# Expert products of the PEER layer: 72 pieces in the 512-column form, their two partial sums added by a DMA

## The chip, the cores and the metric

The kernel runs on one core of a Trainium2 chip. The metric is the device time of one launch in microseconds (us), median over runs. Engines are named as the profile does: PE (TensorE; PEld is its weight load), DVE (VectorE), ACT (ScalarE), POOL (GpSimd), SP (the engine that issues nearly all loads). SPq and POOLq are the DMA queues that SP and POOL issue to.

## What is computed

Three transformer blocks in float32 on 256 tokens of width 1024. The change touches the product with the first expert table in the feed-forward layer (PEER) of the second block:

```python
def peer_ffn(xn, w_q, keys1, keys2, u_tab, v_tab):
    q = (xt @ w_q).reshape(T, PEER_HEADS, PEER_QDIM)
    ...                                    # scores against two key sets, top 16 of each, top 16 of the sums
    gw = jax.nn.softmax(sv, axis=-1)
        u = jnp.take(u_tab, ec, axis=0)    # 16384 experts of 1024 numbers
        act = jnp.einsum('td,thkd->thk', xc, u).astype(f32)
        hact = (jax.nn.gelu(act, approximate=False) * gc).astype(xc.dtype)
        return jnp.einsum('thk,thkd->td', hact, jnp.take(v_tab, ec, axis=0))
```

The kernel gathers nothing. It multiplies all 16384 experts with all 256 tokens, takes the Gelu of every product, multiplies by a weight that is zero for experts not selected, and multiplies with all of the second table.

## The kernel before, in words

**Halves.** Every weight (`raw`, 1 MB chunks of two pieces, 128 x 1024 numbers each) is split for PE in two: ACT copies the rounded number to the high half (L2896, the `hi` of a piece), and DVE (L1543) or POOL (L1431, in `lower`) subtracts it from the weight, which gives the low half `lo`. The activations are kept as two halves as well, `XX`: high ones `xh`, low ones `xl`. A product is hi·xh + hi·xl + lo·xh. Pieces lie in a ring of four buffers `halves`; ACT makes the high half of piece n+3 when PE has read piece n-1. There are up to three `raw` slots; SP loads a slot again when both low halves of its chunk are made.

**The expert stage.** `peer` on PE first makes queries (pieces of the kind `wide`), then 64 small score products (L1246), and then loops over 128 pieces of the table, 128 experts each ("pr.u"). For each, `tile_mms` issues 8 times a product hi·xh (L585) and one hi·xl (L586), and then 8 of lo·xh (L589): 24 products of 256 columns. Two pieces share one of the four PSUM banks of `main`. ACT takes the Gelu of the two pieces at once from PSUM (L3547, `taken`) into `hidden`, 256 columns for each piece; `hidden` fills up to column 32768 of `AR`.

**The other form.** `wide` (used for the queries, and for the gated layers) keeps one bank for a piece. It issues 8 products of 512 columns (L747), which leave hi·xh and hi·xl side by side in the bank, 256 columns each, and 8 of 256 columns that add lo·xh to the first of them (L746); these 8 come before the last of the 512-column ones. The two halves of the bank are then to be added by someone. For the queries ACT copies one half and DVE adds the other.

**Beside the first 72 pieces** (`SELECTED = 72`) DVE selects: `select` does maxima and searches (L2453 to L2458) and then, for the last of it, additions and products of up to 2048 columns (L2480 to L2504), given out in portions of 1750 columns for each piece and finished at piece 72. For those pieces POOL makes the low halves of the odd ones (L1498, L1499), DVE the even ones. From piece 74 on, one-hot matrices are built by DVE, ACT and POOL (L1509), PE multiplies them ("pr.w", L1268), and the weights are applied; DVE makes all low halves from piece 72 on.

**Order.** Each engine runs its instructions in program order. ACT's loop (L3550 to L3567) does for each n: the high half of piece n+3, then for odd n the Gelu of pieces n-1 and n. POOL's loop only makes low halves. `Banks.take` makes PE wait until the bank's last use was emptied.

Of the kernel before, what the change touches and what calls it, by code (L numbers as in the profile page):

```python
# [7 lines left out]
F32 = mybir.dt.float32  # L8
# [3 lines left out]
ALU = mybir.AluOpType  # L12
ACT = mybir.ActivationFunctionType
# [8 lines left out]
SELECTED = 72  # L22
# [264 lines left out]
def weighed_before(f):  # L287

    return groups_of(f).stop
# [16 lines left out]
    "mm",  # L306
]
DMAS = ["ident_in", "cols_in", "const", "x_in0", "x_in1", "pin", "lam_in", "dist_in", "keys_in", "spilled", "refilled", "rg_in", "merge_in",
        "stored", "gb0", "gb1"]


class Program:
# [149 lines left out]
    def unit(self, q):  # L462

        return (self.first[:, 0, 0], self.first[:, 1, 0]) if q == 0 else (self.X[0][:, q % 8, :], self.X[1][:, q % 8, :])

    def hot(self):

# [41 lines left out]
def tensor_engine(k):  # L509

    nc, ps, X, d = k.nc, k.ps, k.X, k.d
    mm, transpose = nc.tensor.matmul, nc.tensor.transpose
    pe, main, aux, s = On(nc.tensor), k.main, k.aux, k.s
# [714 lines left out]
    def peer(prev):  # L1228
        turn_half("pr.x", prev, 0)
        rx = turned_x("pr.x")  # L1230
        B0 = 88 * 256
        qT, k1, k2 = k.ar(B0, 16, 256), k.ar(B0 - 2048, 8, 128), k.ar(B0 - 1024, 8, 128)
        first = four("pr.q", X, rx, lambda: turn_half("pr.x", prev, 1))
        for f in range(4, 16):
            wide(("pr.q", f), main, rx)
            if f == 5:
                turn_back("pr.q", first, (("pr.q", 0), ("pr.q", 2)))
        pe.wait_ge(*k.dma["keys_in"].need(2))
        for j in range(2):
            for sd in range(2):  # L1240
                for h0 in (0, 4):
                    b = main.take(pe, ("pr.s", j, sd, h0))
                    pe.wait_ge(*main.gone(("pr.q", 2)))
                    pe.wait_ge(*main.gone(("pr.q", 7 if h0 == 0 else 15)))
                    for h in range(h0, h0 + 4):
                        ins = mm(ps[:, b, (h - h0) * 128:(h - h0 + 1) * 128],  # L1246
                                 qT[:, 2 * h + sd, j * 128:(j + 1) * 128], (k1, k2)[sd][:, h, :],
                                 start=True, stop=True)
                    filled(("pr.s", j, sd, h0), ins)
        sel = k.AR[:, B0 + 3072:B0 + 3840].rearrange("p (w j n) -> p w j n", w=3, n=128)  # L1250
        OA, OB = k.hot()

        def selected():
            b0, b1 = aux.take(pe, ("pr", "sel", 0)), aux.take(pe, ("pr", "sel", 1))
            pe.wait_ge(*s["vec"].need("pr.sel"))
            for q in range(3):
                bb, oo = (b0, q * 256) if q < 2 else (b1, 0)
                for j in range(2):
                    ins = transpose(ps[:, bb, oo + j * 128:oo + j * 128 + 128], sel[:, q, j], ident[:])
            filled(("pr", "sel"), ins)  # L1260

        def weigh(g):
            b = aux.take(pe, ("pr.w", g))
            pe.wait_ge(*s["prob"].need(("pr.hot", g)))
            pe.wait_ge(*s["pool"].need(("pr.hot", g)))
            pe.wait_ge(*s["act"].need(("pr.hot", g)))
            for q in range(4):
                ins = mm(ps[:, b, q * 128:(q + 1) * 128], OB[:, g % 2, q, :], OA[:, g % 2, q, :],  # L1268
                         start=True, stop=True)
            filled(("pr.w", g), ins)  # L1270

        for n in range(128):
            if n % 2 == 0:
                b = main.take(pe, ("pr.u", n))
            m, hi, lo = weights()
            o = n % 2 * 256
            ins = tile_mms(ps[:, b, o:o + 256], m, hi, lo, X, 0, 8, True, True, rx)
            ins.then_inc(k.piece_read, 1)
            if n % 2:
                k.full["pr.u", n - 1] = k.piece_read, m + 1  # L1280
            if n == SELECTED:
                selected()
            for g in groups_of(n):
                weigh(g)
        down("pr", 128, X, lambda t: [s["part"].need(("pr.v", t))], ring=8)
# [131 lines left out]
def gpsimd_engine(k):  # L1417

    nc, d, dma, s = k.nc, k.d, k.dma, k.s
    gp = On(nc.gpsimd)  # L1420
    load = nc.gpsimd.dma_start
# [3 lines left out]
        gp.wait_ge(*need)  # L1425
        nc.gpsimd.tensor_tensor(dst, src, half[:, 0:src.shape[1]], ALU.pow).then_inc(*s["pow"].mark(name))  # L1426

    def lower(n):
        src, hi, lo = k.piece(n)
        gp.wait_ge(k.hi_made, n + 1)  # L1430
        nc.gpsimd.tensor_tensor(lo, src, hi.bitcast(F32), ALU.subtract).then_inc(k.lo_pool, 1)  # L1431

    def residual(key, row, more):
        def first(j):
# [24 lines left out]
    for h in range(4):  # L1459
        n = 2 * h  # L1460
# [28 lines left out]
    for g in range(8):  # L1489
        n = 2 * g  # L1490
# [4 lines left out]
    B0 = 88 * 256  # L1495
    for j in range(2):
        load(k.ar(B0 - 2048 + 1024 * j, 8, 128), d["keys"][j]).then_inc(*dma["keys_in"].mark(j + 1))
    for n in range(1, SELECTED, 2):  # L1498
        lower(k.u_first + n)  # L1499
    OA, OB = k.hot()  # L1500
    ih1, ih2, gw = k.xsel[:, 0:256], k.xsel[:, 256:512], k.xsel[:, 512:768]
    gp.wait_ge(*k.aux.gone(("pr", "sel", 1)))
# [25 lines left out]
def vector_engine(k):  # L1528

    nc, ps, X, st, x, XN, d = k.nc, k.ps, k.X, k.st, k.x, k.XN, k.d  # L1530
    v, main, aux, s, full = On(nc.vector), k.main, k.aux, k.s, k.full
    te = nc.vector
    step = s["vec"]
# [888 lines left out]
    def peer(prev):  # L2422
        B0 = 88 * 256
        act = k.ar(0, 128, 256)
# [128 lines left out]
        def weighed(g, m):  # L2553

            v.wait_ge(*full["pr.w", g])
            if not weighed_before(m - 2):
                v.wait_ge(*main.gone(("pr.u", m - 2)))
            w = ps[:, aux.of(("pr.w", g)), :].rearrange("p (t i) -> p i t", i=128)
            ts = slice(g * 4, g * 4 + 4)
            te.tensor_tensor(act[:, 0:m, ts], act[:, 0:m, ts], w[:, 0:m], ALU.mult)  # L2560
            te.tensor_copy(act[:, m:128, ts], w[:, m:128]).then_inc(*aux.done(("pr.w", g)))
# [317 lines left out]
def scalar_engine(k):  # L2879
# [624 lines left out]
    def peer(prev):  # L3504
# [33 lines left out]

        def taken(f):

            t = weighed_before(f) * 4
            p = two(main.of(("pr.u", f)))
            a.wait_ge(*full["pr.u", f])
            if t:
                ins = act(p[:, :, 0:t], p[:, :, 0:t], ACT.Gelu)
            if t < 256:
                ins = act(hidden[:, f:f + 2, t:256], p[:, :, t:256], ACT.Gelu)  # L3547
            ins.then_inc(*(s["act"].mark(("pr.h", f)) if t else main.done(("pr.u", f))))

        for n in range(128):  # L3550
            if n == FIRST_HOT - 1:
                a.wait_ge(*aux.gone(("pr", "sel", 1)))
                for need in k.chunk_halved(k.hot_after):
                    a.wait_ge(*need)
                hot(0)
            weights()
            if n == SELECTED - 2:
                w = k.AR[:, B0 + 1536:B0 + 1792]
                a.wait_ge(*s["vec"].need(("pr.sv", 1)))
                act(w, w, ACT.Exp).then_inc(*s["act"].mark("pr.exp"))  # L3560
            for g in groups_of(n):
                if g:
                    hot(g)
            if n == 1:
                a.wait_ge(*full["pr.s", 1, 1, 4])
            if n % 2 and n < 127:
                taken(n - 1)  # L3567
        a.wait_ge(*aux.gone(("pr.w", 63)))
        a.parts = 0
# [377 lines left out]
```

## Time and profile before

| | us |
|---|---|
| device time, median of 3 runs (2816.61 to 3042.89) | 2816.8 |
| span of the profiled execution | 2814.9 |
| PE busy | 2800.3 (99%) |
| DVE busy | 1952.1 (69%) |
| ACT busy | 1624.4 (58%) |
| POOL busy | 345.9 (12%) |

The span is one execution as the hardware profiler saw it; what the device time has beyond it lies before the first and after the last instruction. A share of busy time is an average over all three blocks; the expert stage with its 128 pieces lies from about 1520 to about 1945 us.

### The profile page before, as it was taken

The numbers are of one execution on the slowest core, as the hardware profiler recorded it, in microseconds if no ns is written. First come the engines' busy times: TensorE is split into PE (matmuls) and PEld (weight loads), VectorE is DVE, ScalarE is ACT, GpSimd is POOL, SyncE is SP. The second block draws the span as 40 slices with busy tenths as digits, with TensorE's granted clock in tenths as the row PEclk, the third lists the DMA queues.
The fourth block names the chain that finished last, engine by engine and source line by source line (L and its number), as shares of the span: only waits on it lengthen the run. The fifth ranks groups of instructions, "written<-read, shape, count | busy, mean of one in ns | idle before, by whom it ended". The sixth has DMA issues, their size and how long they took to land.

```text
span 2814.9 us, 42397 instructions
## 1 busy us (share of the span) xinstructions
PE 2800.3 (99%) x16834; PEld 2485.0 (88%) x16834; DVE 1952.1 (69%) x3377; ACT 1624.4 (58%) x2784; POOL 345.9 (12%) x314
## 2 busy tenths in 40 slices
PE   9999999999999999999999999999999999999999
PEld 7888888888988888899889999999888889988997
DVE  6657765776676676768866998677555566766775
ACT  6544655755665564566745445776555555655663
POOL 0000000000010002000002445894000000000000
PEclk9999999999999999999999999999999999999999
DMA  7554556466436555445164554434555574536454
GB/s 229 191 178 159 181 194 227 135 202 221 148 124 194 202 189 181 135 156 187 61 224 166 183 182 160 136 131 161 193 192 193 194 246 137 180 110 209 147 195 149
DMA packets 270485, 491.25 MB, mean 175 GB/s; under 512 B 10880, under 2 KB 181248, under 8 KB 261584
## 3 DMA queue, kind: packets, MB, share of 16 engines
q1 hardware_dynamic: 268864, 480.08, 51.3%
q0 software_dynamic: 1424, 8.45, 0.8%
q8 instruction: 135, 2.21, 0.3%
q14 instruction: 62, 0.51, 0.1%
HBM read 486.41 MB, written 2.10 MB: 174 GB/s over the span
## 4 chain that ended last, share of the span: by engine, by line
PE 94%; DVE 4%; ACT 1%; issue 0%; DMA 0%; POOL 0%; DVEq 0%; POOLq 0%; ACTq 0%
PE ps L659 41%; PE ps L747 11%; PE ps L589 8%; PE ps L585 8%; PE ps L586 8%; PE ps L746 6%; PE ps L606 3%; PE ps L1268 2%; DVE halves L1543 1%; PE ps L1303 1%; PE ps L544 1%; DVE AR L2499 1%; PE ps L952 0%; PE ps L1322 0%; DVE AR L2495 0%
## 5 line engine op out<-in xcount | busy, mean ns | idle before, releaser
L2896 ACT ACTIVATE halves<-raw 128x1024 fp32r<-128x1024 f32 x828 | 870.1, 1058 | 695.5 <-PE ps L659 413.7
L1543 DVE TENSOR_TENSOR halves<-raw,halves 128x1024 fp32r<-128x1024 f32 x790 | 952.9, 1227 | 190.6 <-ACT halves L2896 187.4
L659 PE MATMUL ps<-halves,XX 128*128 128x512 f32 x2628 | 611.6, 391 | 0.4
L659 PEld LDWEIGHTS ps<-halves,XX 128*128 128x128 f32 x2628 | 489.9, 188 | 102.5 <-DVE XX L1581 1.0
L585 PE MATMUL ps<-XX,halves 128*128 128x256 f32 (+1 forms) x1960 | 486.1, 286 | 0.0
L586 PE MATMUL ps<-XX,halves 128*128 128x256 f32 (+1 forms) x1960 | 480.3, 283 | 0.0
L659 PE MATMUL ps<-halves,R 128*128 128x512 f32 x1908 | 439.9, 390 | 0.1
L659 PEld LDWEIGHTS ps<-halves,R 128*128 128x128 f32 x1908 | 356.7, 188 | 73.9 <-issue 0.6
L586 PEld LDWEIGHTS ps<-XX,halves 128*128 128x128 f32 (+1 forms) x1960 | 375.4, 192 | 0.1
L585 PEld LDWEIGHTS ps<-XX,halves 128*128 128x128 f32 (+1 forms) x1960 | 375.0, 191 | 0.1
L747 PE MATMUL ps<-XX,halves 128*128 128x512 f32 x1344 | 338.4, 393 | 0.6 <-DVE XX L1581 0.6
L747 PEld LDWEIGHTS ps<-XX,halves 128*128 128x128 f32 x1344 | 241.7, 189 | 44.5 <-ACT halves L2896 0.9
L589 PE MATMUL ps<-XX,halves 128*128 128x256 f32 (+1 forms) x1960 | 275.3, 283 | 0.2 <-DVE halves L1543 0.2
L589 PEld LDWEIGHTS ps<-XX,halves 128*128 128x128 f32 (+1 forms) x1960 | 252.7, 192 | 0.4 <-DVE halves L1543 0.4
L746 PEld LDWEIGHTS ps<-XX,halves 128*128 128x128 f32 x1344 | 183.2, 190 | 13.4 <-issue 0.4
L746 PE MATMUL ps<-XX,halves 128*128 128x256 f32 x1344 | 187.5, 282 | 0.1
L1426 POOL TENSOR_TENSOR st<-st 128x1 f32<-128x1 f32 x44 | 25.3, 574 | 1182.0 <-DVE st L1608 1001.9
L1431 POOL TENSOR_TENSOR halves<-raw,halves 128x1024 fp32r<-128x1024 f32 x38 | 97.0, 2552 | 435.3 <-ACT halves L2896 435.3
L1558 DVE TENSOR_TENSOR XX<-AR,XX 128x256 fp32r<-128x256 f32 x127 | 53.9, 426 | 137.9 <-ACT XX L3579 137.9
L1509 POOL TENSOR_SCALAR raw<-iota,xsel 128x128 f32<-128x128 f32 x128 | 137.5, 1081 | 34.5 <-PE ps L1268 22.4
L1807 DVE TENSOR_TENSOR AR<-AR,ps 128x256 f32<-128x256 f32 x164 | 68.5, 421 | 81.1 <-ACT AR L3096 81.1
L3096 ACT ACTIVATE AR<-ps 128x256 f32<-128x256 f32 x164 | 61.3, 375 | 89.4 <-PE ps L747 88.0
(390 smaller groups left out, 3180.8 us busy)
## 6 DMA issues: line engine op xcount, KB each, us to landing
raw<-in_w_ffn_in SPq DMA_DIRECT2D x88, 1024.0 KB, 5.1
raw<-in_w_in SPq DMA_DIRECT2D x74, 1024.0 KB, 5.3
raw<-in_uT SPq DMA_DIRECT2D x64, 1024.0 KB, 4.9
raw<-in_peer_v SPq DMA_DIRECT2D x64, 1024.0 KB, 4.9
raw<-in_w_ffn_out SPq DMA_DIRECT2D x44, 1024.0 KB, 4.9
raw<-in_w_up SPq DMA_DIRECT2D x24, 1024.0 KB, 5.8
raw<-in_mlstm_w_in SPq DMA_DIRECT2D x12, 1024.0 KB, 5.2
raw<-in_w_down SPq DMA_DIRECT2D x12, 1024.0 KB, 4.9
```

Of the source, the lines that this page charges most:

```text
L585: mm(o[:, ts], hi[:, q, 0:M], xh[:, k0 + q, ts], start=first and q == 0, stop=False)
L586: mm(o[:, ts], hi[:, q, 0:M], xl[:, k0 + q, ts], start=False, stop=False)
L589: ins = mm(o[:, ts], lo[:, q, 0:M], xh[:, k0 + q, ts], start=False, stop=last and q == a - 1)
L606: ins = mm(ps[:, bs[j], :].rearrange("p (a b) -> p a b", b=128), act[q == 2][:, t, j * 128:(j + 1) * 128], k.halves[:, 0:4, q % 2, t * 128 ...
L659: ins = mm(ps[:, bs[j * (width // 512) + h], :], xv[:, k0 + t, j * 128:(j + 1) * 128], wv[:, t, h * 512:(h + 1) * 512], start=first and q ...
L746: mm(o[:, 0:256], lo[:, p, :], X[0][:, p, :], start=False, stop=False)
L747: ins = mm(o.rearrange("p (h t) -> p h t", t=256), hi[:, q, :], k.XX[:, :, q, :], start=q == 0, stop=q == 7)
L1431: nc.gpsimd.tensor_tensor(lo, src, hi.bitcast(F32), ALU.subtract).then_inc(k.lo_pool, 1)
L1509: nc.gpsimd.tensor_scalar(OA[:, g % 2, q, :], k.iota[:], ih1[:, 4 * g + q:4 * g + q + 1], gw[:, 4 * g + q:4 * g + q + 1], ALU.is_equal, AL ...
L1543: te.tensor_tensor(lo, src, hi.bitcast(F32), ALU.subtract).then_inc(k.lo_made, 1)
L1807: te.tensor_tensor(dst, dst, o[:, 0:256], ALU.add) \
L2896: act(hi, src, ACT.Copy).then_inc(k.hi_made, 1)
```

## The change

For the first 72 pieces PE uses `wide` in place of `tile_mms`. ACT copies the two halves of each bank to a ring for 8 pieces in `AR`, at columns that belong to pieces 72 to 87 of `hidden` (`sides`). For each pair of pieces POOL then issues a DMA from `AR` to `AR` that adds the one half to the other in memory (`summed`, `accum_op=ALU.add`, 256 KB in 1 KB rows, four semaphores in turn), and ACT takes the Gelu of the pair from there, 6 pieces after the pair began. POOL's low halves of the odd pieces are made in four instructions of 256 columns instead of one of 1024. DVE's first weighing no longer waits on a PSUM bank where the piece is one of the 72.

```diff
-        "stored", "gb0", "gb1"]
+        "stored", "u_sum0", "u_sum1", "u_sum2", "u_sum3", "gb0", "gb1"]
...
+    def sides(self, f):
+
+        return self.ar((SELECTED + f % 8 * 2) * 256, 2, 2, 256)
...
-        for n in range(128):
+        for n in range(SELECTED):
+            wide(("pr.u", n), main, rx)
+        for n in range(SELECTED, 128):
...
-    def lower(n):
+    def lower(n, step=8):
         src, hi, lo = k.piece(n)
         gp.wait_ge(k.hi_made, n + 1)
-        nc.gpsimd.tensor_tensor(lo, src, hi.bitcast(F32), ALU.subtract).then_inc(k.lo_pool, 1)
+        for q in range(0, 8, step):
+            ts = slice(q, q + step) if step < 8 else slice(None)
+            ins = nc.gpsimd.tensor_tensor(lo[:, ts], src[:, ts], hi[:, ts].bitcast(F32), ALU.subtract)
+        ins.then_inc(k.lo_pool, 1)
...
-    for n in range(1, SELECTED, 2):
-        lower(k.u_first + n)
+    def summed(f):
+        gp.wait_ge(*k.main.gone(("pr.u", f)))
+        gp.wait_ge(*k.main.gone(("pr.u", f + 1)))
+        parts = k.sides(f)
+        load(parts[:, :, 0], parts[:, :, 1], accum_op=ALU.add).then_inc(*dma[f"u_sum{f // 2 % 4}"].mark(f))
+
+    for n in range(1, SELECTED + 4, 2):
+        if n >= 5:
+            summed(n - 5)
+        if n < SELECTED:
+            lower(k.u_first + n, 2)
...
-                v.wait_ge(*main.gone(("pr.u", m - 2)))
+                v.wait_ge(*(main.gone(("pr.u", m - 2)) if m - 2 >= SELECTED else s["act"].need(("pr.h", m - 2))))
...
         def taken(f):
 
+            if f < SELECTED:
+                a.wait_ge(*k.dma[f"u_sum{f // 2 % 4}"].need(f))
+                act(hidden[:, f:f + 2, :], k.sides(f)[:, :, 0], ACT.Gelu).then_inc(*s["act"].mark(("pr.h", f)))
+                return
...
-            if n % 2 and n < 127:
+            if n % 2 == 0 and 6 <= n <= SELECTED:
+                taken(n - 6)
+            if 1 <= n <= SELECTED:
+                if n >= 9:
+                    a.wait_ge(*s["act"].need(("pr.h", n - 9 - (n - 1) % 2)))
+                a.wait_ge(*full["pr.u", n - 1])
+                act(k.sides(n - 1 - (n - 1) % 2)[:, (n - 1) % 2],
+                    ps[:, main.of(("pr.u", n - 1)), :].rearrange("p (h t) -> p h t", t=256), ACT.Copy) \
+                    .then_inc(*main.done(("pr.u", n - 1)))
+            if n == SELECTED + 1:
+                taken(SELECTED - 4)
+                taken(SELECTED - 2)
+            if n % 2 and SELECTED < n < 127:
                 taken(n - 1)
```

## Rows read from the trace of the kernel before

**Rows 1.** The page: span, then busy time (share) and instructions.

```profile
span 2814.9 us, 42397 instructions
PE 2800.3 (99%) x16834; PEld 2485.0 (88%) x16834; DVE 1952.1 (69%) x3377; ACT 1624.4 (58%) x2784; POOL 345.9 (12%) x314
```

**Rows 2.** Busy by window: stretch, length, each engine, PEclk, DMA share, GB/s.

```profile
1600.00:1640.00 40.00, 40.00 (x335) 40.00 (x335) 35.95 (x89) 18.26 (x21) 18.52 (x7) 1.00 0.55 185
1640.00:1680.00 40.00, 40.00 (x336) 40.00 (x335) 37.81 (x71) 18.26 (x21) 18.41 (x7) 1.00 0.56 185
1680.00:1720.00 40.00, 39.84 (x332) 39.57 (x331) 39.73 (x37) 17.79 (x21) 18.17 (x7) 1.00 0.51 171
1800.00:1840.00 40.00, 40.00 (x344) 40.00 (x343) 28.35 (x67) 31.46 (x73) 35.74 (x39) 1.00 0.40 133
```

**Rows 3.** Chain of work, 1490 to 1960, the longest pieces: start us, us, what.

```profile
1489.97 1.84 PE ps L747 x8
...
1509.53 1.84 PE ps L747 x8
...
1521.98 0.96 PE ps L589 x8
...
1651.58 0.96 PE ps L589 x8
...
1655.52 1.07 ACT halves L2896
...
1671.18 4.24 DVE AR L2499 x6
...
1712.34 1.21 PE ps L589 x8
```

**Rows 4.** Timeline of PE, 1698 to 1735: start us, us, then [idle before <-releaser].

```profile
1712.34 1.21 PE L589 MATMUL ps<-XX,halves 128*128 128x256 f32 x8 [0.16 <-DVE halves L1543]
...
1729.71 1.12 PE L589 MATMUL ps<-XX,halves 128*128 128x256 f32 x8
1730.67 0.82 PE L1259 MATMUL ps<-ident,AR 128*128 128x128 f32 x6
```

**Rows 5.** Timeline of ACT, 1580 to 1600, one pair of pieces.

```profile
1583.46 0.60 ACT L3547 ACTIVATE AR<-ps 128x512 f32<-128x512 f32 x1 [1.76 <-PE ps L589]
1583.95 1.05 ACT L2896 ACTIVATE halves<-raw 128x1024 fp32r<-128x1024 f32 x1
1586.40 1.06 ACT L2896 ACTIVATE halves<-raw 128x1024 fp32r<-128x1024 f32 x1 [1.40 <-PE ps L589]
```

**Rows 6.** Timeline of ACT, 1660 to 1745.

```profile
1737.33 1.06 ACT L2896 ACTIVATE halves<-raw 128x1024 fp32r<-128x1024 f32 x1 [0.82 <-PE ps L589]
```

**Rows 7.** Groups by line and form, ACT, 1480 to 1520: busy us, mean ns.

```profile
L3523 ACT ACTIVATE AR<-ps 128x512 f32<-128x512 f32 x7 | 4.2, 597 | 2.7 <-PE ps L1246 2.7
```

**Rows 8.** Timeline of POOL, 1400 to 1745.

```profile
1579.32 2.40 POOL L1431 TENSOR_TENSOR halves<-raw,halves 128x1024 fp32r<-128x1024 f32 x1 [3.36 <-ACT halves L2896]
...
1665.72 3.72 POOL L1431 TENSOR_TENSOR halves<-raw,halves 128x1024 fp32r<-128x1024 f32 x1 [3.35 <-ACT halves L2896]
...
1734.30 0.60 POOL L1511 TENSOR_SCALAR raw<-iota,xsel 128x128 f32<-128x128 f32 x1
```

**Rows 9.** Groups by line, POOL, whole span: busy us, mean ns | idle before.

```profile
L1426 POOL TENSOR_TENSOR st<-st 128x1 f32<-128x1 f32 x44 | 25.3, 574 | 1182.0 <-DVE st L1608 1001.9 <-DVE st L1629 173.9 <-DVE st L2814 6.3
...
L1464 POOL DMA_DIRECT2D AR<-in_pT x1 | 0.7, 739 | 1.5 <-DVE AR L1635 1.5
...
L1478 POOL DMA_DIRECT2D AR<-in_pT x1 | 0.6, 581 | 1.4 <-DVE AR L1635 1.4
```

**Rows 10.** DMA issues of the whole span: queue, count, KB each, median us to landing.

```profile
raw<-in_uT SPq DMA_DIRECT2D x64, 1024.0 KB, 4.9
...
AR<-in_pT POOLq DMA_DIRECT2D x2, 256.0 KB, 3.0
```

**Rows 11.** Instructions of the tile in_rg: the longest landing in the trace.

```profile
DMA to landing us min/median/max: 7.3/8.9/10.5
```

**Rows 12.** Timeline of DVE, 1655 to 1745.

```profile
1660.86 1.59 DVE L2487 TENSOR_SCALAR AR<-AR 128x128 uint32<-128x128 uint32 x1
1662.49 0.23 DVE L2489 TENSOR_SCALAR AR<-AR 128x128 uint32<-128x128 uint32 x1
...
1664.87 2.29 DVE L2495 TENSOR_TENSOR AR<-AR,iota 128x2048 f32<-128x2048 f32 x1
1667.20 2.85 DVE L2499 TENSOR_TENSOR AR<-AR 128x256 f32<-128x256 f32 x2
...
1700.26 4.31 DVE L2499 TENSOR_TENSOR AR<-AR 128x256 f32<-128x256 f32 x6
...
1711.06 1.23 DVE L1543 TENSOR_TENSOR halves<-raw,halves 128x1024 fp32r<-128x1024 f32 x1
...
1716.88 1.42 DVE L2499 TENSOR_TENSOR AR<-AR 128x256 f32<-128x256 f32 x4
...
1726.35 0.42 DVE L2518 TENSOR_TENSOR AR<-AR,st 128x256 f32<-128x256 f32 x1
```

## The prediction

> **What bounds the kernel now.** The page first: PE is busy for 2800.3 us of a span of 2814.9 [rows 1]. Anything that is to make this kernel faster has to take time from PE or from the few places where PE waits; anything else can only hurt. The windows of the expert stage say who is near PE: up to 1640 us DVE is busy for 36 of 40 us, in 1680:1720 for 39.73, and there PE shows its only loss, 0.16 us; ACT is at 18 and POOL at 18 of 40, the DMA engines at 0.55 [rows 2]. From 1800 on, where the change does nothing, POOL is the fullest after PE, but PE is full. Then the chain of waits: it runs on PE products throughout the stage, except between 1655.5 and 1712 us, where it goes over DVE's selection (L2499 and its like) and comes back to PE at 1712.34 [rows 3]. The timeline of PE has the wait itself: the low-half products of piece 66 start right behind DVE's low half, which ended at 1712.29 [rows 4, 12]. So the stage is PE's, with one stretch of some 57 us in which DVE has no time left over. The median of the runs, 2816.8 us, is 1.9 above the span; I make the sum on the span and add the 1.9.
>
> **PE, the gain.** A narrow piece: 45 pieces lie between the starts of the low-half products at 1521.98 and 1651.58, so 129.60 / 45 = 2.880 us. A piece in the 512-column form: 7 of them between 1489.97 and 1509.53, 19.56 / 7 = 2.794 us [rows 3]. Both stream the same columns (16 x 256 + 8 x 256 against 8 x 512 + 8 x 256); only the per-instruction loss of 8 products goes. 72 x 0.0857 = 6.2 us. This is the same code at the same granted clock of 1.00 a few us earlier in the same trace, so I take it as it is. It is also the whole possible gain, 0.2% of the time, apart from the stalls that stand there now: pieces 0 to 72 take 1729.71 - 1521.98 = 207.73 against 72 x 2.880 = 207.36 [rows 3, 4], 0.4 us.
>
> **DVE, what is given back.** From about piece 46 (the chain leaves PE at 1655.5; (1655.5 - 1522) / 2.88 = 46) to the low half of piece 66, DVE works without a gap. The change takes no work from DVE. Where PE paces DVE, before piece 46, DVE's 10% of idle time absorbs the faster PE; in the 20 pieces after, PE asks for them 20 x 0.0857 = 1.7 us sooner and doesn't get them. In the new form the low half is also wanted earlier within the piece, after 7 of 8 wide products, 7 x 0.23 = 1.61 us (1.84 / 8 = 0.23), in place of 16 x 0.12 = 1.92 us: 0.3 us. Together 2.0 us lost again at pieces 62 to 66. Behind piece 66, DVE catches up; its selection ends at 1726.77 [rows 12], 3.9 us ahead of PE's need at 1730.67 [rows 4]. PE will come 4.2 us sooner, but DVE's own busy stretch begins 4 us sooner too (46 x 0.0857): no wait.
>
> **ACT.** Now a pair of pieces costs ACT 1.05 + 1.06 for the high halves and 0.60 for the Gelu, 2.7 us of 5.76 [rows 5]. After: two copies of 512 columns out of PSUM (0.60 each [rows 7]) and a Gelu of 512 columns out of SBUF; no row has that one, and I take 0.60; its bounds are 0.53 and 1.06, half and all of what 1024 columns out of SBUF take [rows 5]. 2.11 + 1.20 + 0.60 = 3.9 us of 5.59, 4.4 at most: hidden under PE. No table is loaded between copy and Gelu now (Copy of L2896 and Gelu follow each other without one), so none after. At piece 73 two Gelus more (1.2 us) stand on ACT before that of piece 72, at a place where ACT idles 0.8 us soon after [rows 6] and high halves are 3 pieces ahead: nothing.
>
> **POOL, the low halves.** One instruction of 1024 columns takes 2.40 us [rows 8]. For 256 columns with two inputs there is no row. Below, the split is free: 4 x 0.60 = 2.40. Above, the line through the 128 x 1 power (0.574 us [rows 9]) and the 2.40: 0.574 + 255 x 1.786 ns = 1.03, four are 4.1. The line through L1511 (128 columns, 0.60 [rows 8]) and 2.40 at 1024 gives 2.01 ns a column and 0.86, four are 3.4; L1511 is the nearest in kind, so 3.4. The DMA issue: 0.58 and 0.74 us for the same 256 KB in the same rows of 1 KB [rows 9], I take 0.6; that an adding one costs POOL more is not excluded. POOL per pair: 3.4 + 0.6 = 4.0 us, between 3.0 and 4.9, of a period of 5.59. Hidden, 1.6 us to spare.
>
> **Latency of the low half.** Today POOL starts on the low half of piece n right behind ACT's high half, 1.1 us after PE has finished n-4. Now `summed(n-5)` stands before it in program order, and that waits for ACT's copy of piece n-4, which comes after the high half and a Gelu: 1.07 + 0.6 + 0.6 = 2.3, the issue to 2.9, four instructions to 6.3. PE wants it after three pieces and 1.61 us: 3 x 2.79 + 1.61 = 10.0. 3.7 us spare. Behind the low half waits SP with the next load into that `raw` slot: 6.3 + 0.3 + 4.9 to land [rows 10] = 11.5, and ACT takes that chunk when PE has read piece n+1, 5 pieces or 14.0 us after. 2.5 us spare, more for PE, since ACT makes high halves ahead. PSUM: a bank for each piece means PE may be four pieces ahead of ACT's copy, 11.2 us, against 2.3. Nothing waits.
>
> **The landing.** ACT takes a pair's Gelu in the loop four pieces after it copied its second half. The cycle is Gelu, copy, issue, landing, Gelu: L + 1.8 us in 2 x 5.59 = 11.2, so a landing L up to 9.4 us is hidden. The plain 256 KB DMA on the same queue lands in 3.0 us [rows 10]; an adding one reads two streams and meets SP's loads, for which the DMA engines are at 0.55 [rows 2]. No row for adding. Bounds: 3.0, and 10.5, the longest landing of any DMA here [rows 11], 1.6 MB. I take 5. At 10.5: (10.5 + 1.8) / 2 = 6.15 a pair, 36 x (6.15 - 5.76) = +14 us.
>
> **POOL against DVE.** The trace shows that a POOL subtraction and a DVE instruction with two SBUF inputs take turns: POOL's at 1665.72 took 3.72 us in place of 2.40 with DVE's L2495 running until 1667.16, and then DVE's two L2499 took 2.85 where four take 1.42, 0.36 each [rows 8, 12]: 2.1 us lost to DVE. There are eight such losses before piece 66, the first at 1660.86 (1.59 us, where its twin takes 0.23), the last at 1700.26 (six in 4.31) [rows 12]; they sum to 15.7 us. What does the split do? If POOL needs the shared way only for its columns, four times 256 cost DVE what one 1024 costs, and DVE gets in between: 0. If it holds it for its full length, a run of short DVE products loses 3.4 instead of 2.1, 8 x 1.3 = 10.7 us, all of it on PE, since DVE has nothing left there. If it helps as much as it can, it gives the 2.0 + 0.4 us of stalls back. From DVE's end at 1667.16 POOL needed only 2.28 of its 2.40 us, so some of each instruction runs without the way, which speaks for the first; I take 0. The other way round, POOL's four may each wait for a DVE product (0.36, one in eight groups 2.29): 4.0 + 1.4 to 3.4 = 5.4 to 7.4 in that stretch, against 5.59 with 3.7 us spare.
>
> The Trainium skill, SBUF — State Buffer, "Who interferes with whom", has this as a rule: a DVE instruction with two SBUF inputs and a GpSimd one that reads SBUF share a port pair as a lock held for the full instruction. The trace agrees on who meets whom. By the letter of that rule the sum would be the second case, 10.7 us later than the forecast.
>
> **Sum.** -6.2 + 2.0 + 0 = -4.2 us: span 2810.7, device time 2812.6.
>
> **The rivals.**
> *A, DVE loses more to the split instructions.* For it: DVE is at 39.73 of 40 us there [rows 2] and any loss is PE's. Against: the lock is let go between. 2812.6 + 10.7 = 2823.3.
> *B, POOL becomes the bound.* For it: it has two new costs of which neither has a row, and at 4.9 us plus DVE's turns it would be there. It decides from 5.59 us a pair, an issue of 2.2 us. With 4.1 for the low halves and an issue of 2.2: 6.3, 36 x (6.3 - 5.76) = +19: 2836.
> *C, the landing.* Slower than before: a landing of over 9.4 us makes ACT late for everything. It would be clearly slower from (L + 1.8) / 2 = 7.32 us a pair, L = 12.8, over four times the plain one. At 14 us: 7.9, 36 x 2.14 = +77: 2894. Against: even 1.6 MB lands in 10.5.
> *D, the change does not do what it says:* PE gains but another wait of the stage takes all, DVE's being the nearest: 2817, no change. To eat 4.2 us more, DVE's stretch would have to begin 49 pieces before 66, and DVE still idles 10% then.
>
> **How the numbers follow.** Forecast 0.66, A 0.13, B 0.09, C 0.05, D 0.07. The likeliest one's own range: the full 6.2 and the stalls back, 2816.8 - 6.6 = 2810.2, to 1 us of POOL's delays behind D, 2818. The range that holds 8 in 10 takes in A with its price, part of B, and the landing's bound of 10.5 us, 2816.8 + 14 = 2831: 2810 to 2831. Left out: most of B, and C, 0.1 in all. A measurement of this kernel tells from no change about 2%, 56 us; no case gains that, only C beyond 12.8 us and a B of 7.3 a pair lose it. Faster 0.01, same 0.95, slower 0.04.
>
> **What would show it.** PE: L747 and L746 at 2.79 us a piece from 1520 to 1650, no idle before them; if they come at 3 or more, A to C. The end of piece 72 at about 1726.5 in place of 1730.7. POOL: four records of 0.86 (0.6 to 1.03) and one DMA of 0.6 for each pair; idle waiting for ACT (if it idles on nothing, B). The DMA issues: landing of the 36 adding ones around 5 us; ACT's waits should name a DMA nowhere before piece 73 (if they do, C). DVE: L2499 without losses above 2.1 us for each group (A). The forecast is wrong if the stage ends later than at 1730.7, and it is wrong in its reason if it ends sooner while DVE still waits as before.

## The result, and the profile after

| | before | after |
|---|---|---|
| device time, median (us) | 2816.8 | 2837.8 |
| range of the runs of the changed kernel (us) | | 2836.9 to 2839.1 |
| span of the profiled execution (us) | 2814.9 | 2836.9 |
| PE busy (us) | 2800.3 | 2802.0 |
| POOL busy (us) | 345.9 | 399.9 |

The changed kernel is slower: ratio 1.0076, 95% interval 1.0064 to 1.0088, 21 us. It is within the 2% band, but outside the predicted range of 2810 to 2831, and it moved the other way than forecast. The 3042.89 us given above for the kernel before is one execution in a slower state of the chip, which the ratio leaves out.

The windows of the expert stage show where (columns as in [rows 2]: busy us of PE, PEld, DVE, ACT, POOL, then PEclk, DMA share, GB/s):

```profile
1560.00:1600.00 40.00, 40.00 (x232) 35.25 (x231) 37.17 (x137) 26.15 (x37) 28.35 (x35) 1.00 0.84 232
1600.00:1640.00 40.00, 38.06 (x215) 32.38 (x215) 38.52 (x74) 23.42 (x34) 27.47 (x33) 1.00 0.82 224
1640.00:1680.00 40.00, 35.70 (x198) 29.93 (x197) 38.46 (x78) 23.51 (x33) 27.19 (x34) 1.00 0.83 203
1680.00:1720.00 40.00, 34.03 (x182) 28.65 (x183) 39.72 (x34) 19.59 (x27) 22.63 (x29) 0.96 0.67 184
1720.00:1760.00 40.00, 33.19 (x212) 30.17 (x210) 25.59 (x29) 20.77 (x30) 19.17 (x24) 0.91 0.55 145
1760.00:1800.00 40.00, 37.22 (x314) 36.96 (x315) 29.18 (x66) 30.70 (x70) 31.88 (x33) 1.00 0.41 135
```

Up to 1600 us nothing is wrong: PE is full, in the new form. From 1600 on PE loses 2 to 7 us in every 40, and DVE is at 38.5 of 40 already from 1600, where before the change it came near that only at 1680 [rows 2]. Between 1680 and 1760 the granted clock of PE falls to 0.96 and 0.91, behind its longest waits: a price on top. The waits of the stage (engine and line, what it waited for, us, times, longest) name DVE's low halves:

```profile
POOL AR L1511 <- ACT AR L3594: 82.5, 33, 10.4
PEld ps L750 <- DVE halves L1561: 23.6, 13, 6.6
PE ps L750 <- DVE halves L1561: 18.4, 12, 6.2
...
ACT AR L3561 <- DMA AR<-AR: 3.5, 2, 2.5
```

and the chain in 1520:1780 answers to [rows 3]: it was PE's but for 57 us, now its first lines are

```profile
by line: DVE halves L1561 21.7%; DVE AR L2473 13.8%; DVE AR L2471 11.5%; DVE AR L2476 6.8%; DVE AR L2513 6.4%; DVE AR L2517 5.2%; issue 3.9%; DMA raw<-in_uT 3.2%; DMA AR<-AR 3.2%; PE ps L751 2.8%; DVE AR L2522 2.6%; PE ps L1272 2.2%; ACT ha
```

(L751, L750 and L1561 are what L747, L746 and L1543 were before.) DVE has the same instructions as before. What has grown is how long two of them take. Grouped by line, 1520 to 1734, the low half and the 2048-column product; their means in the same window before were 1353 and 2816 ns (the 32 short products of L2499 went the other way, from 755 to 578):

```profile
L1561 DVE TENSOR_TENSOR halves<-raw,halves 128x1024 fp32r<-128x1024 f32 x33 | 61.8, 1872 | 1.0
...
L2513 DVE TENSOR_TENSOR AR<-AR,iota 128x2048 f32<-128x2048 f32 x4 | 16.6, 4140 | 0.1
```

The timelines of POOL and of DVE around 1600 us, where the lag begins, answer to [rows 8, 12]:

```profile
1594.97 1.20 POOL L1511 DMA_DIRECT2D AR<-AR  x1 [1.53 <-ACT AR L3594]
1595.74 3.27 POOL L1439 TENSOR_TENSOR halves<-raw,halves 128x256 fp32r<-128x256 f32 x4
1600.56 1.20 POOL L1511 DMA_DIRECT2D AR<-AR  x1 [1.54 <-ACT AR L3594]
1601.33 3.28 POOL L1439 TENSOR_TENSOR halves<-raw,halves 128x256 fp32r<-128x256 f32 x4
```

```profile
1597.51 1.80 DVE L2494 CAST AR<-AR 128x512 f32<-128x512 uint32 x1
1599.34 2.29 DVE L2498 TENSOR_TENSOR AR<-AR 128x2048 f32<-128x2048 f32 x1
1601.67 4.04 DVE L1561 TENSOR_TENSOR halves<-raw,halves 128x1024 fp32r<-128x1024 f32 x1
```

DVE's low half starts 0.34 us after POOL's four instructions, ends at 1605.71, 1.10 us after the last of them (1604.61), and takes 4.04 us for 1.23 us of work. It did not get in between any of the four. The cast before it likewise ends 0.3 us behind POOL's end at 1599.01 (1.80 for the 0.43 it takes undisturbed). And the split four follow the DMA issue without a gap: they start 0.78 us after it does, 0.43 us before its record ends.

### The profile page after: what moved, and what is told of

Its sections match the earlier page's. It is cut to its first block, busy times and chain, and to the rows that moved or that the text cites. A ratio compares the mean times of both kernels' runs of the same rounds, so it can differ in the third digit from the quotient of the medians.

```text
span 2836.9 us, 41533 instructions
## 1 busy us (share of the span) xinstructions
PE 2802.0 (99%) x16258; PEld 2456.7 (87%) x16258; DVE 1972.0 (70%) x3377; ACT 1659.8 (59%) x2856; POOL 399.9 (14%) x458
## 4 chain that ended last, share of the span: by engine, by line
PE 87%; DVE 9%; ACT 2%; DMA 1%; issue 1%; POOL 0%; SPq 0%; DVEq 0%; POOLq 0%; ACTq 0%
PE ps L663 40%; PE ps L751 12%; PE ps L593 6%; PE ps L589 6%; PE ps L590 6%; PE ps L750 6%; PE ps L610 3%; DVE halves L1561 2%; PE ps L1272 2%; DVE AR L2473 1%; DVE AR L2471 1%; PE ps L1309 1%; DVE AR L2476 1%; DVE AR L2513 1%; PE ps L548 1%
## 5 line engine op out<-in xcount | busy, mean ns | idle before, releaser
L1561 DVE TENSOR_TENSOR halves<-raw,halves 128x1024 fp32r<-128x1024 f32 x790 | 969.3, 1247 | 189.9 <-ACT halves L2914 186.0
L751 PE MATMUL ps<-XX,halves 128*128 128x512 f32 x1920 | 485.7, 394 | 0.8 <-DVE XX L1599 0.8
L751 PEld LDWEIGHTS ps<-XX,halves 128*128 128x128 f32 x1920 | 347.4, 190 | 63.8 <-ACT halves L2914 1.1
L589 PE MATMUL ps<-XX,halves 128*128 128x256 f32 (+1 forms) x1384 | 344.7, 287 | 0.0
L590 PE MATMUL ps<-XX,halves 128*128 128x256 f32 (+1 forms) x1384 | 339.0, 283 | 0.0
L750 PEld LDWEIGHTS ps<-XX,halves 128*128 128x128 f32 x1920 | 261.7, 191 | 42.0 <-DVE halves L1561 23.6
L750 PE MATMUL ps<-XX,halves 128*128 128x256 f32 x1920 | 270.2, 284 | 18.5 <-DVE halves L1561 18.4
L590 PEld LDWEIGHTS ps<-XX,halves 128*128 128x128 f32 (+1 forms) x1384 | 264.7, 191 | 0.1
L589 PEld LDWEIGHTS ps<-XX,halves 128*128 128x128 f32 (+1 forms) x1384 | 264.4, 191 | 0.1
L593 PE MATMUL ps<-XX,halves 128*128 128x256 f32 (+1 forms) x1384 | 194.2, 283 | 0.0
L593 PEld LDWEIGHTS ps<-XX,halves 128*128 128x128 f32 (+1 forms) x1384 | 178.4, 192 | 0.0
L1439 POOL TENSOR_TENSOR halves<-raw,halves 128x256 fp32r<-128x256 f32 (+1 forms) x146 | 124.1, 1167 | 326.4 <-ACT halves L2914 326.4
```

The costliest lines, as they stand in the source:

```text
L589: mm(o[:, ts], hi[:, q, 0:M], xh[:, k0 + q, ts], start=first and q == 0, stop=False)
L590: mm(o[:, ts], hi[:, q, 0:M], xl[:, k0 + q, ts], start=False, stop=False)
L593: ins = mm(o[:, ts], lo[:, q, 0:M], xh[:, k0 + q, ts], start=False, stop=last and q == a - 1)
L750: mm(o[:, 0:256], lo[:, p, :], X[0][:, p, :], start=False, stop=False)
L751: ins = mm(o.rearrange("p (h t) -> p h t", t=256), hi[:, q, :], k.XX[:, :, q, :], start=q == 0, stop=q == 7)
L1439: ins = nc.gpsimd.tensor_tensor(lo[:, ts], src[:, ts], hi[:, ts].bitcast(F32), ALU.subtract)
```

## Experiments

All times are medians beside the kernel before on the same chip (2816.5 to 2816.8), with the ratio to it and its 95% interval. Three theories were on the table for the first twelve: the length of POOL's work, its place in the piece, and the DMAs.

### One instruction for the low half

```diff
-            lower(k.u_first + n, 2)
+            lower(k.u_first + n)
```

> The changed kernel, but POOL makes each low half in one instruction of 1024 columns again. Three theories for the 21 us. Length: the four instructions follow each other without a gap and keep DVE out for 3.27 us in place of 2.40, and DVE's low halves come late; then this run gets back most of the stalls from 1605 us on, 0.87 us for each of some 25 groups: about 2820 us. Place: the low half now waits for ACT's copy and stands behind the DMA issue, so it begins about 2 us later in the piece and falls on DVE's own low half; then this run stays at 2830 or above. DMA: the descriptors and the landing cost; then it stays at 2834 or above.

Measured: 2832.3 us (2831.9 to 2833.4), 1.0057 (1.0040 to 1.0074). 5.6 us back of 21: less than length asked for, more than the others did. POOL's single instruction takes 2.86 us in the mean here where it took 2.40 before; it too stands right behind a DMA issue. It keeps DVE waiting nearly as the four do: over 1520 to 1734 DVE's low half takes 1728 ns in the mean and its 2048-column product 4452 (1872 and 4140 in the changed kernel).

### The split alone

The kernel before, with `lower` in four instructions.

> The kernel before, with POOL's low halves of the odd pieces in four instructions of 256 columns; nothing else. Length theory: DVE loses 0.87 us more at each of the eight meetings before piece 66, where it has no time left: 2822 to 2826 us. Place theory and DMA theory: 2817 to 2819, since the low half begins where it did.

Measured: 2816.2 us, 0.9999 (0.9989 to 1.0009). The split alone does nothing. The length theory falls as told: something in the changed kernel must make the four instructions harmful.

### The low half first, the DMA behind it

```diff
-        if n >= 5:
-            summed(n - 5)
         if n < SELECTED:
             lower(k.u_first + n, 2)
+        if n >= 5:
+            summed(n - 5)
```

> The changed kernel, with POOL making the low half of piece n first and issuing the adding DMA of pair n-5 after it. The low half then waits for nothing but ACT's high half, as before the change. Place theory: the stalls between 1600 and 1670 us go, 2818 us or less. Length theory: little changes, 2832 or above. DMA theory: the DMA is still issued 36 times and lands later, 2834 or above.

Measured: 2825.3 us (2822.7 to 2826.5), 1.0029 (1.0018 to 1.0041). 12.5 us back by order alone, between the theories: DVE's stalls up to 1670 are gone but one of 0.2 us. What is left is one of 3.5 us at 1682, one of 0.7 at 1730 and, at PE, this (start, us, [idle before]):

```profile
1747.11 2.05 PE L1272 MATMUL ps<-raw 128*128 128x128 f32 x8 [5.53 <-ACT raw L3554]
```

ACT is late with the one-hot matrix there, because its Gelus of pairs 68 and 70 stand before it and wait for their sums to land; behind the 5.5 us the same 8 products that take 1.06 us take 2.05: the granted clock is 0.50 in 1747.00:1752.00, 1.2 GHz in place of 2.4.

The order takes the DMA issue away from the front of most low halves, not of all. Where DVE has delayed POOL, the next low half again follows an issue at once and again takes 3.2 to 3.3 us: at 1561, 1606, 1640, 1674 and 1713 us. The first of these lines is such a delay, the last its consequence:

```profile
1667.50 5.55 POOL L1439 TENSOR_TENSOR halves<-raw,halves 128x256 fp32r<-128x256 f32 x4 [1.64 <-ACT halves L2914]
1672.99 1.20 POOL L1511 DMA_DIRECT2D AR<-AR  x1
1673.77 3.26 POOL L1439 TENSOR_TENSOR halves<-raw,halves 128x256 fp32r<-128x256 f32 x4
```

Beside it six short DVE products take 6.29 us where six take 2.1 undisturbed (0.36 each), and the 3.5 us wait of PE at 1682 comes behind them.

### No adding DMA

`summed` is not issued, and ACT's Gelu waits for its own copies: the product with the low half of the activations is left out in the first 72 pieces.

> The changed kernel without the adding DMAs: the Gelu takes the first part alone, so the product with the low half of the activations is missing in the first 72 pieces. POOL's low halves then wait for ACT's high half alone. DMA theory or place theory: near the forecast of 2812 us. Length theory alone: 6 us under the run that only splits POOL's instruction, 2817 to 2820. The 3.4 us stall at piece 76, where ACT waits for the last adding DMA, must be gone under all of them.

Measured: 2810.5 us (2810.1 to 2811.3), 0.9979 (0.9969 to 0.9989). This is the whole of the PE gain, 6.05 us against 72 x 0.0857 = 6.2. Neither the wide form, nor the copies, nor the split costs anything here; the adding DMAs do, by where they stand or by themselves.

### Low half first, in one instruction

> The changed kernel with the low half of piece n first and the adding DMA behind it, and that low half in one instruction of 1024 columns. If the length of POOL's work matters once its place is right, this is faster than the same order with four instructions (2825.3), by up to 8 us; if only the place matters, or if shorter instructions let DVE in between, it is equal or slower, 2825 to 2829.

Measured: 2822.3 us (2820.2 to 2826.1), 1.0021 (1.0011 to 1.0031), 3 us faster than with four. The spread of 6 us is new, and comes with the landing: the median landing is 8.4 us here, the longest 12.5, and ACT waits 16 times for one, 29.5 us in all. DVE's low half takes 1324 ns in the mean and its 2048-column product 2808, against 1728 and 4452 with the same single instruction behind a DMA issue: the issue in front, or the later start that comes with it, costs DVE time with one instruction as well as with four.

### Idle sums in the narrow kernel

The kernel before with 32 adding DMAs behind POOL's low halves, over memory set to zero beforehand.

```diff
+        if 5 <= n < 69:
+            i = (n - 5) // 2
+            gp.wait_ge(k.piece_read, k.u_first + n - 3)
...
+            load(parts[:, :, 0], parts[:, :, 1], accum_op=ALU.add).then_inc(*dma[f"u_sum{i % 2}"].mark(i))
```

> The kernel before (narrow products, one low-half instruction), with 32 adding DMAs of the same shape on POOL's queue, behind the low half of each odd piece, over memory that nobody reads. DMA theory: issuing and descriptors keep DVE out for up to 1.2 us a pair, and the transfers slow SP's loads: 2820 to 2826 us. If it is only the place of the low half and the last landing that cost: 2816 to 2818.

Measured: 2816.6 us, 1.0000 (0.9991 to 1.0010). Issuing them, their descriptors, and 8.4 MB more through the DMA engines cost nothing as long as nobody waits for them and they stand behind the low half. Yet each takes 1.20 us on POOL and lands after 8.3 us in the median. The DMA theory in its plain form falls.

### 68 and 44 wide pieces, low half first

> Low half first, four instructions, but only 68 pieces in the 512-column form; pieces 68 to 71 in the narrow one. The sums of the last pairs then land before ACT comes to the first one-hot matrices. If the wait there (5.5 us of PE at the low-half-first order, and a halved clock behind it) is the landing's, this run gives about 8 us back: 2816 to 2818. If another wait takes its place: 2822 or above.

> Low half first, four instructions, 44 pieces in the 512-column form, the rest narrow: neither the wide products nor the adding DMAs fall in the stretch where DVE has no time left. Theory: what the change costs, it costs there and at the end, so 44 x 0.0857 = 3.8 us are won: 2813 us. If the DMAs cost DVE from the first pair on, it comes late into its busy stretch: 2816 or above.

Measured: 2817.7 us (2813.6 to 2823.6), 1.0004 (0.9994 to 1.0013), and 2817.4 us (2813.1 to 2822.3), 1.0000 (0.9991 to 1.0010). Both spreads are some 10 us; of the 31 executions of the kernel before beside them, 30 keep within 3. The first is 7.7 us below the same order with 72 pieces. In the profiled execution of the first, PE waits for ACT's copies, which stand behind a Gelu that waits for its sum (waits of the stage, then the landings of the DMA's line):

```profile
ACT AR L3562 <- DMA AR<-AR: 59.7, 23, 7.6
```

```profile
DMA to landing us min/median/max: 3.8/8.7/14.5
```

So the stall at the end is the landing's. With it gone, PE waits 6.6 us for ACT's copies, behind landings over the 9.4 us that the prediction allowed in its cycle, and 3.4 us for DVE's low halves; seven of POOL's low halves again stand directly behind a DMA issue. For 44 pieces the expectation of 2813 us missed. In its profiled execution (2816.5) PE waits 0.36 us for a copy of ACT and 1.60 and 0.32 us, at 1681 and 1711, for low halves of DVE: some of the price is still paid in DVE's busy stretch, where no sum is issued any more. What makes the times of these two runs spread is not shown.

### The later start, without a DMA

As the run without DMAs, with POOL waiting for ACT's copies of pieces n-5 and n-4 before the low half of n.

> As the run without adding DMAs (2810.5), but POOL's low half of piece n waits until ACT has copied piece n-4 out of PSUM, as it does in the changed kernel; no DMA is issued, and the Gelu again takes the first part alone. Place theory: the late low half alone pushes DVE behind: the DVE stalls of the changed kernel come back, 2824 to 2832 us. If it takes the DMA issue or its descriptors to do that: 2810 to 2813.

Measured: 2811.4 us (2811.0 to 2815.8), 0.9984 (0.9974 to 0.9994). Starting 2.3 us after PE's piece in place of 1.1 costs 0.9 us, and the place theory falls for four instructions between which DVE gets in. For one instruction, or for four that keep DVE out, the later start was not run without a DMA.

### The landing given more room

64 wide pieces, low half first, and

```diff
-            if n % 2 == 0 and 6 <= n <= WIDE + 4:
-                taken(n - 6)
+            if n % 2 == 0 and 8 <= n <= WIDE + 6:
+                taken(n - 8)
```

with the low half in one instruction, and in four:

> Three changes to the changed kernel at once: low half first and in one instruction; the Gelu of a pair 8 pieces after it began in place of 6, so that a landing of up to 15 us is hidden; 64 pieces in the 512-column form, so that the last landings are past before the one-hot matrices. If place and landing were all that cost: 64 x 0.0857 = 5.5 us less 2 us for DVE's busy stretch, 2812 to 2814 us, with little spread. If the transfers cost something else: 2816 or above.

> The same with POOL's low halves in four instructions. If shorter instructions let DVE in between, equal or up to 1 us faster than with one; if length matters, slower by 1 to 3 us.

Measured: 2810.9 us (2810.3 to 2812.2), 0.9980 (0.9971 to 0.9990), and 2815.5 us (2812.7 to 2816.8), 0.9996 (0.9987 to 1.0006). The first beats both kernels, by 5.7 us (the one before, beside it) and by 27 us: of 64 x 0.0857 = 5.5 us all is there. Its landings are longer than in the runs before (9.3 us in the median) and nobody waits for them (0.6 us in all). With four instructions 4.6 us are lost again. There PE waits for DVE's low halves at 1690, 1696 and 1708, and the 32 products of 256 columns on DVE (L2518) take 911 ns in the mean against 687. In this trace too POOL falls behind, and the low halves at 1599, 1635, 1668 and 1684 stand 0.8 us behind a DMA issue and take 3.3 us, though the order puts the DMA behind; with one instruction none does.

### The changed kernel's own order, with 68 wide pieces

> The changed kernel in its own order (adding DMA before the low half, Gelu 6 pieces after), with 68 wide pieces instead of 72. It takes away only the last landings in front of the one-hot matrices. If that stall (3.4 us at PE) is a loss of its own: 2833 to 2834 us. If DVE's lag hides it: 2837 or more.

Measured: 2830.4 us (2829.2 to 2831.6), 1.0050 (1.0033 to 1.0067). Without the last two sums 7.5 us are back, more than the 3.4 us of the wait itself. How much of that is the landing's is not shown: between the two profiled executions PE's waits for DVE's low halves fall from 18.4 to 13.5 us as well, and their longest from 6.2 to 2.3. What remains against the run without DMAs, 20 us, is DVE's: PE waits for its low halves 12 times, 13.5 us, from 1606 us on as in the changed kernel; the rest includes products at a lowered clock (0.96 in 1680:1720).

### What is it about a DMA in front?

Left open were the rest of the delay, and the issue directly in front of POOL's instructions: in the changed kernel POOL's first instruction starts 3.4 us after ACT begins the high half, 2.2 in the run above. Three runs: e13 is the changed kernel with this edit; e14 has no DMA, waits for ACT's copies and sets all 1024 columns to zero instead of one; e15 is the narrow kernel with idle sums in front:

```diff
         if n >= 5:
             summed(n - 5)
         if n < SELECTED:
+            if n >= 5:
+                gp.wait_ge(k.hi_made, k.u_first + n + 1)
+                nc.gpsimd.memset(k.piece(k.u_first + n)[2][:, 0:1, 0:1].bitcast(F32), 0.0).then_inc(*s["pool"].mark(("step", n)))
+                gp.wait_ge(*s["pool"].need(("step", n)))
             lower(k.u_first + n, 2)
```

> The changed kernel, its own order, with one more POOL instruction (one column set to zero) between the adding DMA and the low half, and a wait of POOL for it, so that the low half begins when all of POOL is done with the DMA issue. It makes the low half later still, by some 0.5 us. Theory of the closed block: right behind a DMA issue POOL's four instructions keep DVE out until the last, with the wait between them DVE gets in again: 2825 us or less. Theory of the later start: no better than 2836, rather worse.

> No adding DMA (the Gelu takes the first part alone), the low half waits for ACT's copy as in the changed kernel, and POOL then first sets the 1024 columns to zero, which delays the low half by 0.5 to 1.5 us (the trace will say how much) without reading anything. Later-start theory: DVE's stalls come back, 2825 or more. Closed-block theory: 2811 to 2814.

> The kernel before with 32 adding DMAs over memory that nobody reads, each issued directly in front of the low half (four instructions), which begins some 0.8 us later than before. Closed-block theory: DVE is shut out for 3.3 us a time wherever it meets POOL, 2820 to 2830 us. Otherwise: 2816 to 2818, as with the DMAs behind the low half.

Measured: e13 2834.3 us (2833.7 to 2836.2), 1.0062 (1.0045 to 1.0078); e14 2810.6 us (2810.3 to 2810.7), 0.9978 (0.9968 to 0.9988); e15 2832.7 us (2830.6 to 2836.9), 1.0054 (1.0037 to 1.0071).

e15 is the cause by itself: the kernel before, no wide form, no copies, nobody waiting for the sums. Against the kernel before it has idle sums and the split; idle sums behind the low half cost nothing, nor did the split alone (2816.6 and 2816.2). With the DMA issue in front of the split low half it is 16 us. PE waits 11.1 us for DVE's low halves in the profiled execution, 5.4 and 5.2 of them at a time, and the granted clock is 0.88 in 1680:1720. Its POOL and DVE rows look like the changed kernel's:

```profile
1606.58 1.20 POOL L1514 DMA_DIRECT2D AR<-AR  x1 [1.71 <-ACT halves L2912]
1607.36 3.27 POOL L1433 TENSOR_TENSOR halves<-raw,halves 128x256 fp32r<-128x256 f32 x4
```

```profile
1607.53 4.20 DVE L1559 TENSOR_TENSOR halves<-raw,halves 128x1024 fp32r<-128x1024 f32 x1
```

e14 says that delay by itself is not it: with a memset of 0.95 us the low half begins 3.2 us after ACT begins the high half, nearly the 3.4 of the changed kernel, and it is as fast as without. There a DVE product of 2048 columns that meets POOL's four instructions loses 0.42 us (2.71 for 2.29), and POOL's take 6.05 us instead:

```profile
1595.56 6.05 POOL L1439 TENSOR_TENSOR halves<-raw,halves 128x256 fp32r<-128x256 f32 x4
```

```profile
1596.62 2.71 DVE L2502 TENSOR_TENSOR AR<-AR 128x2048 f32<-128x2048 f32 x1
```

e13 missed its number and still shows the mechanism. With the wait between, DVE gets in again (the same product takes 2.71 us while POOL's four take 5.98), no PE wait names DVE any more, and the engine that PE waits for is now POOL, 12.7 us: 1.20 for the DMA, 0.55 for the one column, and 2.8 to 6.9 for the four, into which DVE gets, are often over the 5.6 us of a pair. ACT then waits 49.5 us for chunks of the table, which SP loads only when POOL is done. So no run gives the 20 us back by letting DVE in alone.

```profile
1642.56 2.07 PE L750 MATMUL ps<-XX,halves 128*128 128x256 f32 x8 [4.59 <-POOL halves L1439]
```

## Why the prediction was wrong, point by point

**PE's gain, right.** 6.2 us predicted; 6.05 us measured where no sum is issued, 5.7 of 5.5 in the version with 64 pieces. Nothing was hidden there. The stalls that stand now, 0.4 us in the prediction, are 0.5: 1521.98 is the start in the chain, and the same product starts at 1521.82 in the timeline that 1729.71 is from.

**DVE gives 2.0 us back, wrong in size.** It gave back about 0.2 us. The step left DVE no slack at all in its busy stretch. With 64 pieces and the low half in one instruction, where the split can't have helped, PE waits for DVE nowhere.

**ACT, right.** A copy takes 0.58 and a Gelu out of SBUF 0.61 us; ACT is not late but for what it waits for.

**POOL's low halves, right in length, 2.83 us** against 3.4 (bounds 2.40 and 4.1), 3.27 behind a DMA issue. **The DMA issue, wrong:** 0.6 predicted from plain ones [rows 9], 1.20 measured; 0.78 of it before the next instruction starts. Together 4.05 us a pair, the 4.0 of the sum. POOL was not the bound in the changed kernel (rival B), only in the run with an extra instruction.

**POOL against DVE: the step that failed.** It is the term of 0 in the sum -6.2 + 2.0 + 0, and it measured 20: an estimated 14 of them with POOL's low half in one instruction already (2832.3 - 7.5 - 2810.5), the other 5.6 with the split (2837.8 - 2832.3).

The step weighed only whether the split holds the shared way for its columns or for its length, took 0, and put the other case at 10.7 us (8 x 1.3 is 10.4). Both cases were about POOL's instructions among themselves. Measured: four instructions by themselves let DVE in between (0.42 us lost, split alone -0.3 us). Behind a DMA issue they close into one block of 3.27 us. That the DMA stands directly in front was in the change part of the prediction, but as delay, under "Latency of the low half". It allowed 2.9 us to POOL's start, which came at 3.4; where DVE could get in between, that delay was indeed harmless (0.9 us, and nothing at 3.2).

Rival A named the place and the engine, DVE's loss, but neither its cause nor its size, 20 us and not 10.7. Two things in the trace go with the larger size: DVE's own low half meets the block in nearly every pair from 1602 to 1665 us, not only eight times after 1655; and behind its longest waits PE runs at half its clock for a while. Behind the 6.2 us of waiting that end at 1728.5 the granted clock is 0.50 in 1728.50:1731.00, and the products of one piece take 2.07 and 3.56 us in place of 1.12 and 2.00. Of the 28.0 us between the spans with and without sums, PE's waits are 21.8 (18.4 for DVE's low halves, 3.4 at the end); the other 6.2 are, by my estimate, mostly such slower products.

```profile
1728.50 2.07 PE L750 MATMUL ps<-XX,halves 128*128 128x256 f32 x8 [6.16 <-DVE halves L1561]
1730.37 3.56 PE L751 MATMUL ps<-XX,halves 128*128 128x512 f32 x8
1733.77 1.12 PE L750 MATMUL ps<-XX,halves 128*128 128x256 f32 x8
1734.73 0.63 PE L751 MATMUL ps<-XX,halves 128*128 128x512 f32 x2
```

**The landing, right for the middle, wrong for the end.** 5 us taken, 6.6 in the median (3.8 to 9.6), hidden under 9.4; ACT waits only for the last two, 1.1 and 2.5 us. But the sentence on piece 73 counted two Gelus of 0.6 us and "nothing": it left out that they wait for sums issued last, at a place where the one-hot matrices stand behind them on ACT: 3.4 us of waiting in place of nothing, and at most the 7.5 us by which the version with 68 pieces is faster. And with the low half in front of the DMA, landings of up to 14.5 us did pass the bound of rival C; in the run with 68 pieces PE waits 6.6 us behind them.

**The sum as measured:** 2810.5 without sums, + 20 (DMA issues in front, mostly at DVE), + 7.5 (the last two sums, their landing and more) = 2838. It is split by runs: each term is a difference of two, and the last holds some of DVE's waits.

**What stays open.** Why the block closes. POOL's DMA record of 1.20 us overlaps the first instruction behind it by 0.43, and the four then take 0.44 us longer than by themselves. The Trainium skill, GPSIMD Engine Reference, "Instruction dispatch", says that consecutive instructions are no barrier between the eight cores of GpSimd, and in "When to use GPSIMD" that a pair of them writes a DMA's descriptors. Then two cores would run 0.44 us behind the other six through all four instructions, one or the other would always be reading, and the way would never be free. That e13, which makes all wait once, opens the block again fits, and the overlap fits; it is an argument, no run saw the cores. Nor was the narrow kernel run with a DMA in front of a single instruction: there DVE has nothing to get in between of, yet the wide form with one instruction is 10 us slower with the DMA in front (2832.3) than behind (2822.3). So the closing of the four explains why the split brought no relief, but not all of the loss. A rival for the rest stands untested: work of POOL that DVE can't enter, one instruction or a closed four, may cost more merely because it starts later in the piece; the two runs with a late start and no DMA had four instructions that let DVE in.

## What to carry to other kernels

On POOL, place a DMA issue behind the arithmetic that somebody waits for, not in front of it, when DVE works with two SBUF inputs beside it; and make sure in the trace that POOL doesn't fall so far behind that the issue stands in front of the next piece after all. Splitting POOL's instructions gained nothing here: 0.3 us by itself, within the noise, and with adding DMAs behind the low half it lost 3.0 and 4.6 us. Give an adding DMA more time to land than a plain one (here 9 us in the median and up to 16, against 3 for the two plain ones, which load the same size in other stages of the kernel), and look where its last user stands at the end of the loop. Here the two together, with the low half in one instruction and 64 pieces in place of 72, turn 2837.8 into 2810.9 us, 5.7 below the kernel before.

## What was not expected of the hardware

An adding DMA of 256 KB in rows of 1 KB costs POOL 1.20 us to issue where a plain one costs 0.58 to 0.74, and its 9.4 MB took 22.7% of the DMA engines' time in 1500:1770 where 42.9 MB of loads took 48.1%: twice as much per byte.

```profile
q1 hardware_dynamic: 5870, 42.85, 48.1%
q0 software_dynamic: 9792, 9.44, 22.7%
```

The Trainium skill, SBUF — State Buffer, "Who interferes with whom", has the lock held for one full instruction. The traces agree for instructions by themselves (0.42 us of waiting inside four of 0.7), and show a group of four held as one behind a DMA issue (4.04 us for 1.23 of work).
